# Expert products grouped by their stationary part, and rounded products in the opening run of unread products, in a two-layer streaming encoder on Trainium2

## The reference, cut to what matters

```
def swiglu(h, w1, w3, w2):
    return (jax.nn.silu(h @ w1) * (h @ w3)) @ w2

def moe_ffn(h, router_w, router_b, w1, w3, w2):
    logits = h.astype(jnp.float32) @ router_w.astype(jnp.float32) + router_b.astype(jnp.float32)
    top_v, top_i = lax.top_k(logits, TOP_K)
    top_w = jax.nn.softmax(top_v, axis=-1)
    combine = jnp.sum(jax.nn.one_hot(top_i, N_EXPERTS, dtype=jnp.float32) * top_w[..., None], axis=-2)
    y = jnp.zeros_like(h)
    for e in range(N_EXPERTS):
        y = y + combine[..., e:e + 1] * swiglu(h, w1[e], w3[e], w2[e])
    return y
```

```
    c_act = jax.nn.silu(c)
    for l in range(DEPTH):
        mod = c_act @ w_mod[l] + b_mod[l]
        sh1, sc1, g1, sh2, sc2, g2 = jnp.split(mod, 6, axis=-1)
        h = modulate(rms_norm(x, norm_mix[l]), sh1, sc1)
        proj = h @ w_in[l]
```

## Time and profile before

| | |
|---|---|
| median of three executions | 1535.81 us |
| profiled execution, first to last instruction | 1535.7 us |
| PE busy | 1515.2 us (99%), 7785 products |
| DVE busy | 1298.2 us (85%) |
| ACT busy | 968.0 us (63%) |
| DMA | 494.13 MB, mean 322 GB/s |
| expert products, L1323 to L1325 | 4032 of 128x512 |
| mean granted TensorE clock | 0.996 |

### The profile page before, as it was taken

How to read it: one execution, slowest core, us unless ns; L and a number is a source line. 1 busy time by engine, 2 the same in 40 slices (tenths; PEclk the granted TensorE clock), 3 DMA queues, 4 the chain that set the end, 5 groups by cost and what they waited for, 6 DMA issues and landing times.

```text
span 1535.7 us, 19169 instructions
## 1 busy us (share of the span) xinstructions
PE 1515.2 (99%) x7785; PEld 1236.0 (80%) x7785; DVE 1298.2 (85%) x1175; ACT 968.0 (63%) x841; POOL 90.3 (6%) x141
## 2 busy tenths in 40 slices
PE   8999999999999999999999999999999999999997
PEld 4886799999788568888888888888888888888885
DVE  5888887778885579988899999898998888998996
ACT  3532444444554357777777777787777787777775
POOL 5300100000000030100000100000010000000000
PEclk9999999999999999999999999999999999999999
DMA  9776698877823199999999999999999999999990
GB/s 347 285 254 239 231 359 323 304 288 274 310 94 131 55 312 391 377 385 386 354 363 385 369 392 391 354 364 382 367 390 376 376 357 375 382 364 372 411 368 30
DMA packets 161862, 494.13 MB, mean 322 GB/s; under 512 B 4587, under 2 KB 8855, under 8 KB 161767
## 3 DMA queue, kind: packets, MB, share of 16 engines
q1 hardware_dynamic: 156160, 474.76, 82.7%
q0 software_dynamic: 4928, 16.69, 3.1%
q10 hardware_dynamic: 678, 1.40, 0.2%
HBM read 483.91 MB, written 8.91 MB: 321 GB/s over the span
## 4 chain that ended last, share of the span: by engine, by line
PE 90%; DVE 6%; SPq 2%; DMA 1%; ACT 1%; issue 0%; DVEq 0%; ACTq 0%
PE bank L1323 20%; PE bank L1324 20%; PE bank L1325 20%; PE bank L975 4%; PE bank L1183 4%; PE bank L1224 3%; PE bank L1223 3%; PE bank L1222 3%; PE bank L972 2%; PE bank L1356 2%; PE bank L1198 1%; PE bank L1199 1%; PE bank L1200 1%; DMA ring<-in_w_mod_dram 1%; DVE ring_low L2044 1%; PE bank L998 1%
## 5 line engine op out<-in xcount | busy, mean ns | idle before, releaser
L2044 DVE TENSOR_TENSOR ring_low<-ring,w_high 128x2048 fp32r<-128x2048 f32 x336 | 768.6, 2293 | 95.1 <-ACT w_high L2547 89.0
L2547 ACT ACTIVATE w_high<-ring 128x2048 fp32r<-128x2048 f32 x336 | 646.6, 1926 | 228.8 <-PE bank L1325 220.3
L1323 PE MATMUL bank<-w_high,x_high 128*128 128x512 f32 x896 | 352.9, 394 | 0.1
L1324 PE MATMUL bank<-ring_low,x_high 128*128 128x512 f32 x896 | 351.4, 392 | 0.0
L1325 PE MATMUL bank<-w_high,x_low 128*128 128x512 f32 x896 | 348.9, 389 | 0.0
L1323 PEld LDWEIGHTS bank<-w_high,x_high 128*128 128x128 f32 x896 | 168.5, 188 | 37.4 <-DVE ring_low L2044 1.2
L1325 PEld LDWEIGHTS bank<-w_high,x_low 128*128 128x128 f32 x896 | 168.2, 188 | 37.4
L1324 PEld LDWEIGHTS bank<-ring_low,x_high 128*128 128x128 f32 x896 | 168.3, 188 | 34.7
L1323 PE MATMUL bank<-w_high,act_high 128*128 128x512 f32 x448 | 178.8, 399 | 0.2 <-DVE ring_low L2044 0.2
L2468 ACT ACTIVATE tmp_r<-ring 128x1024 fp32r<-128x1024 f32 x84 | 88.9, 1061 | 140.8 <-PE bank L1224 82.0
L1324 PE MATMUL bank<-ring_low,act_high 128*128 128x512 f32 x448 | 177.7, 397 | 0.0
(11 more groups left out here) (381 smaller groups left out, 1657.3 us busy)
## 6 DMA issues: line engine op xcount, KB each, us to landing
ring<-in_moe_w_dram SPq DMA_DIRECT2D x168, 2048.0 KB, 9.1
ring<-in_w_mod_dram SPq DMA_DIRECT2D x23, 2048.0 KB, 12.9
ring<-in_ffn_w_dram SPq DMA_DIRECT2D x21, 2048.0 KB, 11.8
ring<-in_w_in_dram SPq DMA_DIRECT2D x7, 2048.0 KB, 13.6
ring<-in_w_out_dram SPq DMA_DIRECT2D x4, 2048.0 KB, 8.4
ring<-in_w_in_dram SPq DMA_DIRECT2D x4, 1024.0 KB, 15.5
ring<-in_w_mod_dram SPq DMA_DIRECT2D x2, 1024.0 KB, 15.7
gate_row<-in_b_mod_dram POOLq DMA_DIRECT2D x4, 512.0 KB, 7.6
```

Source lines behind the costliest of these rows:

```text
L1323: mm(out_, x_h, w_h, start=first, stop=False)
L1324: mm(out_, x_h, w_l, start=False, stop=False)
L2044: tt_(moe_low(u, m // 2)[:, c], moe_slot(u, m // 2)[:, c], w_high[:, m % HIGHS, :].bitcast(F32), ALU.subtract).then_inc(low_made, 1)
L2547: act(w_high[:, m % HIGHS, :], moe_slot(u, m // 2)[:, c], ACT.Copy).then_inc(high_made, 1)
```

## The change

Two things are changed.

First, in `up` and `down` the six products of a row block (three for each column half) are issued by their stationary part: the four with the high part, then the two with the low part. In `down` the row block becomes the outer loop, so that both halves of a row block stand together. The number of products, their operands and the sums are the same; `last_down` stays as it was, and so does the last column group of `up`, which has one half.

Second, `keep_clock` at the start runs 7 of its 11 float32 products, and a new function `keep_clock_rounded` runs 23 rounded ones behind them, which read `h_high`. DVE fills `h_high` with a constant at the very start, and waits before `norm_x(0)` until these products have read it, because `xn` lies at the same place.

```
@@ in the program of PE
+            def keep_clock_rounded():
+                still = lambda k, n: h_high[:, k, 0:n]
+                wide_ = lambda k: h_high[:, k:k + 2, :].rearrange("p k t -> p (k t)")
+                for b, k, n, moving in ([(6, 0, P, wide_(2))] * 3
...
+                                        + [(6 + i % 2, 0, P, wide_(2)) for i in range(4)]):
+                    ins = mm(bank[b][0:n, 0:moving.shape[1]], still(k, n), moving, start=True, stop=True)
+                ins.then_inc(s_steady_read, 1)
@@ up
                             for kk in range(per):
                                 k = (2 * half + part) * per + kk
                                 for jj in range(n_j):
-                                    c = slice(jj * W, (jj + 1) * W)
-                                    ins = three(bank[first + jj][:, :], x_high[:, u % 2, k, :], x_low[:, u % 2, k, :],
-                                                w_h[:, kk, c], w_l[:, part * per + kk, c], k == 0, k == KB - 1)
+                                    c, o = slice(jj * W, (jj + 1) * W), bank[first + jj][:, :]
+                                    mm(o, x_high[:, u % 2, k, :], w_h[:, kk, c], start=k == 0, stop=False)
+                                    mm(o, x_high[:, u % 2, k, :], w_l[:, part * per + kk, c], start=False, stop=False)
+                                for jj in range(n_j):
+                                    c, o = slice(jj * W, (jj + 1) * W), bank[first + jj][:, :]
+                                    ins = mm(o, x_low[:, u % 2, k, :], w_h[:, kk, c], start=False, stop=k == KB - 1)
@@ down
-                        for half in range(2):
-                            c = slice(half * W, (half + 1) * W)
-                            for bb in range(HB // 2):
-                                hb = part * HB // 2 + bb
-                                h = slice(hb * P, (hb + 1) * P)
-                                ins = three(bank[4 + half][:, :], act_high[:, j % 2, h], act_low[:, j % 2, h],
-                                            w_h[:, bb, c], w_l[:, hb, c], j == 0 and hb == 0,
-                                            j == NJ - 1 and hb == HB - 1)
+                        for bb in range(HB // 2):
+                            hb = part * HB // 2 + bb
+                            h = slice(hb * P, (hb + 1) * P)
+                            for half in range(2):
+                                c, o = slice(half * W, (half + 1) * W), bank[4 + half][:, :]
+                                mm(o, act_high[:, j % 2, h], w_h[:, bb, c], start=j == 0 and hb == 0, stop=False)
+                                mm(o, act_high[:, j % 2, h], w_l[:, hb, c], start=False, stop=False)
+                            for half in range(2):
+                                c, o = slice(half * W, (half + 1) * W), bank[4 + half][:, :]
+                                ins = mm(o, act_low[:, j % 2, h], w_h[:, bb, c], start=False,
+                                         stop=j == NJ - 1 and hb == HB - 1)
@@ PE, start of the program
-            keep_clock(bank[6], consts[:, 0:2, :].rearrange("p a n -> p (a n)"), 11)
+            keep_clock(bank[6], consts[:, 0:2, :].rearrange("p a n -> p (a n)"), 7)
+            eng.wait_ge(s_steady, 1)
+            keep_clock_rounded()
@@ DVE, start of the program
+            nc.vector.memset(h_high[:, :, :].bitcast(F32), 0.37).then_inc(s_steady, 1)
             eng.wait_ge(pre_a.sem, pre_a.at("c"))
             mod_part(0, 0, (0,))
+            eng.wait_ge(s_steady_read, 1)
             norm_x(0)
```

More of the change, by code:

```diff
@@ L401, in hybrid_stream_block @@
         s_const = sem("constants_made")
+        s_steady = sem("steady_operands_made")
+        s_steady_read = sem("steady_operands_read")
         s_out = sem("out_stored")
@@ L924, in keep_clock @@
                     mm(b[:, 0:src.shape[1]], ident, src, start=True, stop=True)
+            def keep_clock_rounded():
+                still = lambda k, n: h_high[:, k, 0:n]
+                wide_ = lambda k: h_high[:, k:k + 2, :].rearrange("p k t -> p (k t)")
+                for b, k, n, moving in ([(6, 0, P, wide_(2))] * 3
+                                        + [(6, i % 2, P, wide_(2 + 2 * (i % 2))) for i in range(4)]
+                                        + [(6, 0, 96, wide_(2))] * 3 + [(6, 0, 66, wide_(2))] * 3
+                                        + [(6, 0, P, h_high[:, 2, :])] * 3 + [(6, 0, 66, h_high[:, 2, :])] * 3
+                                        + [(6 + i % 2, 0, P, wide_(2)) for i in range(4)]):
+                    ins = mm(bank[b][0:n, 0:moving.shape[1]], still(k, n), moving, start=True, stop=True)
+                ins.then_inc(s_steady_read, 1)
             def row_sum_wide(l, which, b):
```

## The result

The changed kernel took 1543.90, 1544.10 and 1544.54 us, median 1544.1, against 1535.81 before. The ratio is 1.0047, 95% interval 1.0029 to 1.0066: slower by half a percent, clear of the noise, and above the range of 1535.0 to 1540.5. The profiled execution has a span of 1542.8 us (before 1535.7).

A forecast was written before the change was run, and what follows sets the result against it. The prediction took TensorE (PE), busy nearly all the time, as the bound: 1535.7 + 0 for the experts + 2.6 for the start = 1538.3 us, 0.16% slower, counted as the same; range 1535.0 to 1540.5 us.

The forecast's parts named there:

- The experts' term: Expert products in `up` and `down`: the new order leaves their spacing unchanged, 0 us, taken between -5 and +9 us.
- The prediction's own sign of being wrong: In the changed kernel's profile, a distance in `up` under 0.228 or over 0.231 us would show the forecast wrong.
- The difference between `up` and `down`: Expert loops: usual distances some 0.229 and 0.233 us, put down to the operands (another stationary tile) and left there.
- Rival 4: Expert products: alternating banks and repeats cost 0.004 us on 2304 products, +9 us, 1547 us; chance 0.03.
- Rival 1: Expert products: repeated stationary operands save their weight load, 15.7 us, giving 1522.6 us; chance 0.10 for both forms.
- smaller form: Expert products: `down` falls to the spacing of `up`, -5 us, 1533 us; its chance is within 0.10 for both forms.
- The start: Unread products at the start: the first read product begins 2.87 us later, net 2.6 us later kept to the end.
- rival 3: Start: DVE's fill of `h_high` hinders POOL writing PE's constants, 0.8 us moving all PE work, 1539.1 us; chance 0.12.
- the 0.28 us at the chunk products: Second group of chunk products: PE's wait for DVE, 1.37 us against 1.09 for sixteen products, goes.
- Rival 5: Start: the delay is hidden, since first weights or constants were the bound, 1535.8 us; chance 0.08.
- The clock (rival 2): Half-clock falls, 1.7 us each: one missed 1536.6, both 1534.9, chance 0.20; one added 1540.0, chance 0.12.
- The base: Whole kernel: the sum started from the span of 1535.7 us, taken as 0.1 us under the median time.

The follow-up runs named there:

- e4_banks_alternate: Kernel before with only the order in `up` changed: the column half, and with it the bank, changes at every product, repeats as before; 1533.83 us.
- e8_one_repeat: Kernel before with `up` reordered so the stationary tile repeats once in six products, and `down` alternating its two row blocks product by product; 1535.89 us.
- e9_four_same_weights: Kernel before with two-bank `up` products reordered: x_high stationary four times in line, weights' tiles in the same sequence of kinds; 1537.46 us against 1536.25.
- act_with_w_high: Kernel before with padding alone moving act_high and act_low by 160 bytes, to the place of w_high within 256 bytes (192); 1530.53 us, ratio 0.9954.
- one_place: Kernel before with padding alone, so x_high, x_low, w_high, act_high and act_low begin at ring_low's place within 256 bytes (128); 1524.61 us, ratio 0.9915.
- e1_order_only: Kernel before with the new order of the expert products alone, start as it was; 1542.81 us against 1536.01, ratio 1.0035.
- e2_start_only: Kernel before with the longer run of unread products at the start alone (7 float32, 23 rounded), old expert order; 1538.61 us against 1536.01, ratio 1.0003.
- weights_one_place: Kernel before with padding putting w_high and ring_low at 128, all four stationary tiles at 192, both orders in one kernel; 1545.34 us against 1536.04.

## Why the prediction was wrong, point by point

**The experts' term, the step that failed.** The prediction took 0 between -5 and +9, because "bank and repeats are shown to do nothing". Both halves were right: e4_banks_alternate cleared the banks, e8_one_repeat and e9_four_same_weights the repeats. What failed is the inference that the order then has no third property. It has: in which sequence the two weights' tiles stream. All rows that I compared had one and the same sequence, h l h h l h: the one-bank and the two-bank group of `up`, and `down` too. They could not show its price. It is 5.4 us over `up` and 1.3 over `down`, and it is there only because w_high and ring_low stand at different places (192 and 128): with both at 128 it is gone. The prediction's own sign of being wrong, a distance in `up` over 0.231 us, came: 0.2317.

**The difference between `up` and `down`**, 0.229 and 0.233, was put down to "another stationary tile" and left there. The stationary tile was indeed what differed, and it was the lead: of the tiles that `down` reads act_with_w_high moved nothing but that one, and `down` went from 233.4 to 229.1 ns, 5.3 us over its distances. A spacing that differs between loops of the same shape asked for an explanation by something that neither order nor shape has, the address.

**Rival 4** had the outcome that came, a longer spacing in `up`, +9 us on 2304 products where 5.4 came in `up` and 6.5 in all, but not the mechanism: it put the price on alternating banks and repeats, which cost nothing. It had 0.03, since no row spoke for it; the honest reading was that no row spoke against it either, for the order was in none.

**Rival 1**, repeats pay, is excluded, and so is that they cost: with the weights' sequence of before, one repeat in six and three, with a run of four, both stand at 229.0 ns, and in the layout of one_place two and four repeats both at 226.8. Its smaller form, `down` falling to the spacing of `up`, did not come either: `down` rose by 1.1 ns.

**The start** was right: 14 passes, 23 rounded products, L904 at 15.31 for 15.44 forecast, DVE's fill and POOL not in each other's way (rival 3: PE began at 4.58, not later than 4.60), the 0.28 us at the chunk products gone, as forecast. Rival 5 is out: the first projection begins at 37.77 for 35.02, 2.75 us later.

**The clock (rival 2)** moved as that rival said it might: two falls missed, one added. Over the profiled executions, +2.74 at the start grew to 4.0 us by 99 us, fell to 2.3 and then 0.8 where the two falls of before are missing, and grew in the experts to 7.3. The base was off too: the sum set the span of 1535.7 equal to the median time of 1535.81, but times are 1.6 to 1.8 us above spans, so the profiled execution of the kernel before took some 1537.4 (an estimate) and was slower than its median by 1.6. In medians of times the change is 6.8 for the order and 2.6 for the start, from e1_order_only and e2_start_only, in means 5.9 and 0.7; their sums, 9.4 and 6.6, lie on both sides of the 8.3 measured.

## What to carry to other kernels

When rows are to show that an order is free, look what they hold constant: here every row streamed its two weights' tiles in the same sequence. When two loops of the same shape have different spacing, compare the addresses of their operands before their order: 384 bytes of padding gave 11.6 us, the worst layout cost 9.6, and the worst order 6.8. And an execution with other clock falls is no comparison for 3 us; lay the traces over each other product by product in the stretch that is asked about.

## What the runs showed of the hardware

The spacing of a rounded product with 512 columns at full clock is not a constant. It went from 226.8 ns (all operands at one place within 256 bytes) over 229.0 (stationary tile and w_high at one place, ring_low 64 bytes off), 230.8, 232.9 and 233.3 to 235.0 ns, with the same instructions. By the Trainium skill (TensorE: Matmul & The Clock Gate, Step-by-step: what each phase is for) PE has two independent read ports, and loading the next tile does not take read bandwidth from the running product. The runs here don't agree with that: between before and act_with_w_high nothing differs for `down` but the address of the loaded tile, and its spacing falls by 4.3 ns; between before and weights_one_place the tokens stay at 192 and w_high goes from there to 128, and `up` rises by 4.3. So the loaded tile and the streamed one are not independent. How they meet stays open: that it is reads of one memory part at a time is a guess that no run tests. The eight combinations of places measured don't give a rule for unequal ones, and why one sequence of the weights' tiles costs 2.7 ns more than another, with as many changes between them, is not shown.

In which of its executions the clock falls, and where, differs for one and the same kernel. The spans of the kernel before were 1532.2 to 1540.7 us in one comparison, with a mean granted clock of 0.998 and 0.993.
